# Layer 1 of an expert mixture: the picks in the last 32 key rows done as plain products over their 4096 experts instead of gathered

## The reference

```python
def peer_ffn(h, w_query, sub_keys, u_tab, v_tab):          # per 128 tokens
    q = (hc @ w_query).reshape(128, 8, 2, 64)               # 8 heads, 2 halves
    s = jnp.einsum('chpd,hpnd->chpn', q, sub_keys)          # 128 scores a half
    s_top, i_top = lax.top_k(s, 16)
    cand = s_top[:, :, 0, :, None] + s_top[:, :, 1, None, :]
    cand_id = i_top[:, :, 0, :, None] * 128 + i_top[:, :, 1, None, :]
    best, pos = lax.top_k(cand, 16)                         # 16 experts a head
    eid = take_along_axis(cand_id, pos)                     # 128 experts a token
    gate = softmax(best)
    act = gelu(einsum('chkd,cd->chk', u_tab[eid], hc)) * gate
    return einsum('chk,chkd->cd', act, v_tab[eid])
```

## Time and profile before

| What | us |
|---|---|
| Median of three runs | 3532.21 (3530.38 to 3534.53) |
| Span of the profiled execution | 3317.3 |
| Median less that span, outside the recorded work | 214.9 |
| PE busy | 2336.2 (70%) |
| DVE busy | 1679.4 (51%) |
| POOL busy | 1480.8 (45%) |
| ACT busy | 558.5 (17%) |

### The profile page before, as it was taken

The page is one execution under the profiler, slowest core; times in us unless marked ns, Lnnn a source line. Parts: engine busy times, 40 slices in busy tenths (PEclk is TensorE's granted clock), DMA queues, the critical chain, the costliest instruction groups (busy, mean ns, idle before and its releaser), DMA issues.

```text
span 3317.3 us, 36982 instructions
## 1 busy us (share of the span) xinstructions
PE 2336.2 (70%) x12540; PEld 1281.0 (39%) x12540; DVE 1679.4 (51%) x4368; ACT 558.5 (17%) x1179; POOL 1480.8 (45%) x1577
## 2 busy tenths in 40 slices
PE   7899867898999888995465444447898545444444
PEld 5477624365777545764121000004587400000000
DVE  2521576644233586436965444443712795444444
ACT  2320231401100235102240000002511210000000
POOL 1100044444444444430666777771000167777775
PEclk9999978799999898997575555557899755555555
DMA  8967679899999896991999999993233299999998
GB/s 307 352 209 267 238 269 350 304 354 378 362 365 366 323 347 235 363 334 64 375 349 388 409 409 409 409 409 111 70 114 134 84 379 409 409 409 406 409 409 341
DMA packets 325915, 1047.22 MB, mean 316 GB/s; under 512 B 27424, under 2 KB 38752, under 8 KB 325728
## 3 DMA queue, kind: packets, MB, share of 16 engines
q0 software_dynamic: 240192, 880.90, 69.2%
q1 hardware_dynamic: 85536, 163.95, 14.1%
HBM read 1043.70 MB, written 1.05 MB: 315 GB/s over the span
## 4 chain that ended last, share of the span: by engine, by line
PE 49%; DVE 18%; issue 13%; DMA 10%; ACT 3%; PEld 3%; POOL 2%; PEldq 0%; DVEq 0%; ACTq 0%; POOLq 0%
PE ps L404 24%; PE ps L440 12%; DVE UV L1044 8%; DMA UV<-in_v_tab,idxT 7%; PE ps L426 4%; PEld ps L404 3%; ACT arena L1679 2%; PE ps L396 2%; DMA W<-in_w_mod 2%; POOL UV L2157 1%; PE ps L529 1%; PE ps L571 1%; DVE arena L1415 1%; DVE arena L1424 1%; DVE arena L1418 1%
## 5 line engine op out<-in xcount | busy, mean ns | idle before, releaser
L1044 DVE SCALAR_TENSOR_TENSOR UV<-ps,UV 128x1024 f32<-128x1024 f32 x768 | 909.8, 1222 | 833.4 <-PE ps L426 816.3
L2157 POOL DMA_INDIRECT UV<-in_u_tab,idxT x768 | 723.5, 942 | 1182.4 <-DVEq L1510 498.1
L440 PE MATMUL ps<-UV,acts 128*32 128x512 f32 x3072 | 632.5, 908 | 560.3 <-DVE acts L1053 456.6
L2167 POOL DMA_INDIRECT UV<-in_v_tab,idxT x768 | 724.9, 944 | 281.6 <-issue 198.8
L404 PE MATMUL ps<-H,W 128*128 128x256 f32 (+2 forms) x3296 | 668.7, 363 | 36.4 <-ACT H L1679 26.5
L404 PEld LDWEIGHTS ps<-H,W 128*128 128x128 f32 (+1 forms) x3296 | 574.7, 194 | 147.3 <-issue 76.6
L404 PE MATMUL ps<-arena,W 128*128 128x256 f32 (+1 forms) x1632 | 371.6, 385 | 20.4 <-issue 8.6
L440 PEld LDWEIGHTS ps<-UV,acts 128*32 128x32 f32 x3072 | 78.3, 129 | 716.1 <-DVE acts L1053 572.7
L404 PEld LDWEIGHTS ps<-arena,W 128*128 128x128 f32 (+1 forms) x1632 | 304.4, 190 | 103.3 <-issue 53.2
L426 PE MATMUL ps<-hs,selb 32*128 32x512 bf16 x1536 | 208.5, 530 | 153.1 <-DVE UV L1044 153.0
L1679 ACT ACTIVATE gel<-dots 128x2 f32<-128x2 f32 x384 | 77.4, 202 | 1255.9 <-DVE UV L1044 1247.3
(11 more groups left out here) (198 smaller groups left out, 1698.9 us busy)
## 6 DMA issues: line engine op xcount, KB each, us to landing
W<-in_w_in SPq DMA_DIRECT2D x30, 2048.0 KB, 10.1
UV<-in_w_mod POOLq DMA_DIRECT2D x18, 2048.0 KB, 12.3
W<-in_w_ff SPq DMA_DIRECT2D x16, 2048.0 KB, 14.2
UV<-in_w_ada POOLq DMA_DIRECT2D x9, 2048.0 KB, 11.7
W<-in_w_out SPq DMA_DIRECT2D x8, 2048.0 KB, 11.4
W<-in_w_mod POOLq DMA_DIRECT2D x6, 2048.0 KB, 19.9
W<-in_w_query SPq DMA_DIRECT2D x6, 2048.0 KB, 9.2
UV<-in_u_tab,idxT POOLq DMA_INDIRECT x768, 8.8
```

Source lines behind the costliest of these rows:

```text
L440: last = mm(ps[q:q + GROUP, YB, :], acts[:, tok % SLOTS, GROUP - 1 - r:2 * GROUP - 1 - r], Vs[:, tok % SLOTS, hf * 512:(hf + 1) * 512], st ...
L1044: dve.scalar_tensor_tensor(out=Us[:, j, :], in0=ps[:, b:b + 2, :].rearrange("p a b -> p (a b)"), scalar=1.0, in1=Us[:, j, :], op0=MUL, op1 ...
L2157: pool.indirect_dma_start(Us[:, j, :], None, A["u_tab"], off).then_inc(sem(f"u_arrived{j}"), 16)
L2167: pool.indirect_dma_start(Vs[:, j, :], None, A["v_tab"], off).then_inc(sem(f"v_arrived{j}"), 16)
```

## The change

Key rows 96 to 127 of layer 1 (DROWS = 32, D0 = 96) are taken out of the gathers of tiles 4 and 5. For tokens from 512 on, both gathers get a bound: an index above it (experts 12288 and up of layer 1) is to be passed over without an error, and the slot keeps what it held. The gates used with the gathered rows are kept in two new tiles, gates_even and gates_odd, in which the gates of the passed-over picks are zero; gateT keeps the full gates. Since a slot may now hold old rows, `dot` no longer writes its product over them: its output goes to the PSUM banks that it read. This holds for all 768 tokens, the other layer too.

The passed-over picks are computed by a new function `dense`, placed after the routing of tile 5 and its rows, in front of `close_stream`. It has three parts.

1. Marks, 64 times for 4 tokens each. DVE builds a one-hot of each pick's second key (colhot, 128 by 4 by 128), a one-hot of its first key among the 32 rows (rowhot, 128 by 4 by 32), and multiplies the latter by the gates. PE multiplies the two (4 products), which gives for each token a 32 by 128 map of gates. After every 16 tokens ACT copies the maps, PE transposes them, and ACT writes them to G (128 experts of a row on partitions; 32 rows; 256 tokens).
2. Rows, 32 times. PE transposes the 128 experts of a key row of u_tab (8 transposes), ACT copies them, and PE multiplies them by H (8 products of 128 by 128 by 256). ACT takes the gelu of two rows at once and DVE multiplies by the map in G.
3. Outputs, in 4 quarters of 256 features. PE multiplies the rows of v_tab by G (32 products of 256 columns for each of two halves of a quarter, 256 in all), and DVE adds the sums to X.

The tables' last quarters come through the weight ring as 16 chunks of 2 MB: 8 of u_tab in rows of 4 KB, 8 of v_tab in pieces of 1 KB. Beats stand between all parts, with a pace of their own (DPACE = 3.2 us of estimated work a visit).

The core of the diff:

```diff
+DROWS = 32
+D0 = NKEY - DROWS
+DPACE = 3.2
@@ the chunks
+        def dense_chunks(tag):
+            at = LAYER[tag] * NEXP + D0 * NKEY
+            for c in range(DROWS // 4):
+                chunk(("du", tag, c), rows(A["u_tab"][at + 512 * c:at + 512 * c + 512, :]), 4, D)
+            for q in range(QUARTERS):
+                for c in range(DROWS // 16):
+                    chunk(("dv", tag, q, c), rows(A["v_tab"][at + 2048 * c:at + 2048 * c + 2048, :])[:, :, 256 * q:256 * q + 256], 16, 256)
@@ PE
+                for b in range(MARKS):
+                    pe.wait_ge(sem("picks_marked"), nxt("picks_marked"))
...
+                    for q in range(MARKED):
+                        last = mm(o[32 * q:32 * q + 32, b % 4 * P:(b % 4 + 1) * P], rowhot[:, b % 2, q, :], colhot[:, b % 2, q, :],
+                                  start=True, stop=True)
...
+                    dense_beat(0.9)
...
+                turn_rows_of(0)
+                for r in range(DROWS):
+                    if r + 1 < DROWS:
+                        turn_rows_of(r + 1)
+                    pe.wait_ge(sem("rows_turned"), nxt("rows_turned", 2))
...
+                    for k in range(DT):
+                        last = mm(o[:, r % 2 * SEQ:(r % 2 + 1) * SEQ], turned[r % 2][:, k, :], H[:, k, :], start=(k == 0), stop=(k == DT - 1))
...
+                    dense_beat(5.0)
...
+                        for e in range(2):
+                            for r in range(16):
+                                i = 16 * c + r
+                                last = mm(o[e][:, 0:SEQ], w[:, r, e * P:(e + 1) * P], G[:, i, :], start=(i == 0), stop=(i == DROWS - 1))
+                                if r == 7:
+                                    dense_beat(3.6)
...
+                            dense_beat(3.6)
+            dense("x1")
             close_stream(1)
@@ DVE
-                    dve.scalar_tensor_tensor(out=Us[:, j, :], in0=ps[:, b:b + 2, :].rearrange("p a b -> p (a b)"), scalar=1.0,
-                                             in1=Us[:, j, :], op0=MUL, op1=MUL, accum_out=dots[:, j:j + 1]).then_inc(sem("dots"), 1)
+                    both = ps[:, b:b + 2, :].rearrange("p a b -> p (a b)")
+                    dve.scalar_tensor_tensor(out=both, in0=both, scalar=1.0, in1=Us[:, j, :], op0=MUL, op1=MUL,
+                                             accum_out=dots[:, j:j + 1]).then_inc(sem("dots"), 1)
+                def mark(b):
...
+                    dve.tensor_tensor(out=colhot[:, b % 2, :, :], in0=iotak.unsqueeze(1).to_broadcast([P, MARKED, P]),
+                                      in1=colT[:, four].unsqueeze(2).to_broadcast([P, MARKED, P]), op=ALU.is_equal)
+                    link(dve.tensor_tensor(out=rowhot[:, b % 2, :, :], in0=iotak[:, D0:].unsqueeze(1).to_broadcast([P, MARKED, DROWS]),
+                                           in1=rowT[:, four].unsqueeze(2).to_broadcast([P, MARKED, DROWS]), op=ALU.is_equal))
+                    dve.tensor_tensor(out=rowhot[:, b % 2, :, :], in0=rowhot[:, b % 2, :, :],
+                                      in1=wide(gateT)[:, four].unsqueeze(2).to_broadcast([P, MARKED, DROWS]),
+                                      op=MUL).then_inc(sem("picks_marked"), 1)
@@ POOL
+            def bound(tok):
+
+                return {"bounds_check": NEXP + D0 * NKEY - 1, "oob_is_err": False} if tok >= 4 * P else {}
-                    pool.indirect_dma_start(Us[:, j, :], None, A["u_tab"], off).then_inc(sem(f"u_arrived{j}"), 16)
+                    pool.indirect_dma_start(Us[:, j, :], None, A["u_tab"], off, **bound(tok)).then_inc(sem(f"u_arrived{j}"), 16)
```

More of the change, by code:

```diff
@@ L234, in two_blocks_kernel @@
         hp2 = view(9232, D, dt=bf16)
+        G = view(0, DROWS, SEQ)
+        colhot = view(8192, 2, MARKED, P)
+        rowhot = view(9216, 2, MARKED, DROWS)
+        colT = view(9472, 2 * P)
+        rowT = view(9728, 2 * P)
+        iotak = view(9984, P)
+        turned = [view(8192 + 1024 * i, DT, P) for i in range(2)]
+        beside_g = [varb, rstd]
         NBANK, HB, YB = 8, 0, 4
@@ L468, in beat @@
                 owed[0] += us
-                while owed[0] >= PACE and seen[0] < min(segment[1], PAIRS * ready[0]):
-                    owed[0] -= PACE
+                while owed[0] >= pace[0] and seen[0] < min(segment[1], PAIRS * ready[0]):
+                    owed[0] -= pace[0]
                     visit(seen[0])
@@ L2041, in rows_after, with dense, dense_beat, copy_marks @@
                     beat("rows", n, s)
+            def dense(tag):
+                unit = counter()
+                def dense_beat():
+                    beat("dn", tag, unit("unit"))
+                def copy_marks(f):
+                    evac(("dm", tag, f), beside_g[f % 2][:, :])
+                    act.sem_inc(sem("marks_copied"), 1)
+                def set_marks(f):
+                    p = full_bank(act, ("dt", tag, f))
+                    link(A_(G[:, :, BLOCK * f:BLOCK * f + BLOCK], p.rearrange("p (t r) -> p r t", r=DROWS)))
+                    act.sem_inc(free(("dt", tag, f)), 1)
+                    act.sem_inc(sem("marks_set"), 1)
+                def copy_turned(r):
+                    if r > 1 and r % 2 == 0:
+                        act.wait_ge(sem("rows_scored"), nxt("rows_scored"))
+                    elif r > 1:
+                        full_bank(act, ("ds", tag, r // 2 - 1))
+                    for a in range(2):
+                        evac(("du", tag, r, a), wide(turned[r % 2][:, 4 * a:4 * a + 4, :]))
+                        act.sem_inc(sem("rows_turned"), 1)
+                def gelu_rows(i):
+                    if i > 1:
+                        act.wait_ge(sem("dense_acts"), nxt("dense_acts"))
+                    evac(("ds", tag, i), beside_g[i % 2][:, :], f=ACT.Gelu_apprx_tanh)
+                    act.sem_inc(sem("dense_gelus"), 1)
+                for b in range(MARKS):
+                    if b % 4 == 2 and b > 4:
+                        set_marks(b // 4 - 1)
+                    dense_beat()
+                    if b % 4 == 3:
+                        copy_marks(b // 4)
+                set_marks(MARKS // 4 - 1)
+                dense_beat()
+                copy_turned(0)
+                for r in range(DROWS):
+                    if r + 1 < DROWS:
+                        copy_turned(r + 1)
+                    if r and r % 2 == 0:
+                        gelu_rows(r // 2 - 1)
+                    dense_beat()
+                gelu_rows(DROWS // 2 - 1)
+                for _ in range(8 * QUARTERS * DROWS // 32):
+                    dense_beat()
             def first_norm():
```

126 lines of the change are left out of this document (121 added, 5 removed).

## The result

The changed kernel takes 3653.99 us (median of 4 runs, 3649.71 to 3661.51) against 3531.3 for the kernel before on the same chip: ratio 1.0365 [1.0343, 1.0387], 123 us slower. Forecast were +30, in a range that ended at 3635. The sign was right, the size was not.

What follows compares the result with a forecast made beforehand. Transfers were taken to bound the kernel before, with POOL 3% behind. Marks 121, rows 262, outputs 180 and tail 20 made 583 us against 553, +30: 3562 us, range 3526 to 3635 for 8 in 10.

Steps and rivals of the forecast that it cites:

- What bounds the kernel before: Closing 108 pairs: transfers fill the whole period, 5.12 us a pair; POOL's four gathers, 4.96 us, lie 3% below.
- the 214.9 us outside of it I leave as they are: Whole kernel: 214.9 us of the time lie outside the profiled span and stay, so span 3347 becomes 3562 us.
- Gathers: Layer 1, bounded gathers: transfers drop to 3.71 us a pair; POOL stays at 1.24 us a gather, floor 4.96 a pair.
- the upper bound of 1.34: POOL's time for a bounded gather: at most 0.10 us above 1.24, for a costlier test of each index.
- Rival A: Gathers in rows and outputs: POOL's work shrinks with the rows moved, 0.98 us a gather; 3535 us, chance 0.18.
- Rows: 32 dense rows with 51 visits: POOL 253 us, PE 245, DMA under 230, plus 9 for misfits: 262 us.
- Outputs: Dense outputs with 35 visits: POOL 174 us, PE 166, DMA 171 to 220; taken as 180 us.
- The price of 50 us for pieces of 1 KB: Outputs' table loads, 16.8 MB in 1 KB pieces: 41 us by bytes, 90 by packets, 50 taken.
- Marks: 64 marks at 1.16 us with 18 visits at 2.46 us, DVE working in order: 121 us.
- Dot product to PSUM: DVE's dot product written to PSUM: no difference taken, at most 0.1 us an instruction.
- rival C: Rows and outputs: PE's clock falls to 0.8 (sign: below 0.9 in the rows); 3622 us, chance 0.12.
- D: Gathers: POOL gets slower, 1.34 us a gather, 5.36 a pair; 3595 us, chance 0.10.

Runs made afterwards that it cites:

- e09_before_again: The kernel before, unchanged, profiled on a late chip (single gathers come late): 3556.94 us in its one run.
- e17_idle_bound: The kernel before with a bound on every gather that no index exceeds, so all rows move; late chip: ratio 1.0031 against the kernel before.
- e01_before: The kernel before, unchanged, profiled on a quick chip (409 GB/s): 3330.53 us, span 3328.8.
- e07_gelu_first: The changed kernel with ACT taking the GELU of two scored rows before copying the next turned row; late chip: ratio 1.0289 against the kernel before.
- e16_after_again: The changed kernel, unchanged, run on a quick chip: ratio 1.0299 against the kernel before.
- e15_gelu_first_again: The changed kernel with ACT's GELU ahead of the next turned row's copy, run on a quick chip: ratio 1.0248 against the kernel before.
- e02_bound_only: The changed kernel without its dense part, keeping bounded gathers, zeroed gates and dot product in PSUM; quick chip: ratio 1.0024 against the kernel before.

## Why the prediction was wrong, step by step

**What bounds the kernel before: right for its profile, wrong for the times.** The transfers fill the pair in the profiled execution. The 5.12 us were 553 us over 108 pairs, but 107 steps lie between the first dot products of pairs 276 and 383, 5.18 us each; no term of the forecast's sum rests on the difference. The times shown were of a late chip, where single gathers set the pair. The step "the 214.9 us outside of it I leave as they are" failed: 2 us lie outside, and the rest is inside, 70 us of it behind the first dot product of pair 276 (642.3 us to the end in e09_before_again and 642.4 in e17_idle_bound, 571.9 in e01_before). The gap of 6% between span and median was itself the hint that the profile was taken under other conditions than the times.

**Gathers: right in kind, the floor too low.** Passed-over rows cost the engines almost nothing, and POOL becomes the floor. But 1.24 us was taken as unchanged where it is 1.295; the upper bound of 1.34 held it. Over 86 pairs of rows and outputs that is 19 us. Rival A is out: with rows passed over a gather takes more than before, not less. The Trainium skill (DMA: Bandwidth & Descriptors, section SWDGE vs HWDGE vs iDMA) ties GpSimd's work to descriptors it computes; here the trace shows no such dependence: a gather costs 0.99 us whether it moves all its rows (e17_idle_bound) or 72% of them.

**Rows: this step failed, 262 against 310 and 356 us.** It compared totals, POOL 253, PE 245, DMA under 230, took the largest and added 9 us "for each load or wait of PE's that misfits". On the quick chip the parts are: POOL's floor 264 in place of 253 (the measured 262 without loads has no misfit in it at all); the loads 30; ACT's order 17. The DMA engines had time for the loads on average, as the sum said, but a load does not wait for the gaps: it delays the gathers beside it, and a POOL at its floor never gives that back. And the 2 us stop for the scored bank was in the diff (one bank, and a copy of the next row ahead of the GELU that frees it), not in the sum, which knew of no such dependence. On the late chip, as an estimate from runs on three chips: 51 x 5.84 = 298, and with the 30 of the loads it makes 328, what e07_gelu_first shows; ACT's order adds 28 to 37. How the loads cost there was not measured.

**Outputs: 180 against 191 and 235.** On the quick chip POOL's floor is 181, without loads the stage takes 186.5 (183 with half the products) and with them 192; the bound of 171 to 220 held. The price of 50 us for pieces of 1 KB was beside the point, since the loads cost the stage 5. On the late chip 35 x 5.84 = 204; less 5 for loads, some 25 us are left that no run took apart.

**Marks: 121 against 128 and 137.** The work was right to a few us; DVE's waits for spread between marks and visits were not in it.

**Dot product to PSUM: "no difference" cost 5 us.** The bound of 0.1 us an instruction covered it.

The balance for late chips: forecast +30; rows +94, outputs +55, marks +16, end -2; less the 70 us by which the kernel before is dearer there in the same stretch: +123. Measured +123. On the quick chip +30, +48, +11, +7 and -5 make +91; e16_after_again shows +100 by the medians and 92.5 between its span and that of e01_before.

Would a sound level have saved the range? That is within the noise: its upper end was 3635 / 3532 = 1.029, and the quick chip gave 1.0299 [1.0277, 1.0321]. The sign set for rival C did appear on late chips (a clock of 0.86 in the rows, below the 0.9 that was named; 0.93 on the quick chip), but its mechanism did not: with half the products the clock fell to 0.79 and the rows took 322 us against 328. D was right in kind and half right in size: POOL got slower by 0.055 us a gather, not 0.10, and that explains 19 us of the miss.

No version beat the kernel before. The nearest with the dense part whole, e15_gelu_first_again, is 2.5% slower. The reason is in e02_bound_only: the change frees 27% of a resource behind which, 3% away, stands another that it slows, and pays for it with new work that takes 380 us by itself (80.5 + 184.8 + 114.0, ACT's order included) and must be hidden beside 108 pairs.

## What to carry to other kernels

Before you free a full resource, take the next one's period from the timeline and price what the edit does to that one: here 3% was the whole prize, and the edit's own bound test ate it. When two streams share a resource, do not compare totals with a maximum; ask which of them is in order at its floor, because it adds every delay that the other causes. And when the span and the timed runs differ by more than a few us, take it that the profile and the times come from different conditions, and look for the stretch that shows which.

## What was not expected of the hardware

- A gather with a bound costs POOL 0.99 us instead of 0.94, at any number of passed-over rows; each of these is still a packet, under 512 B.
- The same program has 409 or about 355 GB/s in the same stretch, each chip keeping its level in all its runs, and differs by 6% in its time. On the late chips DVE waits up to 10.9 us for a gather's rows, and the pair stays at 5.84 us with 27% of the bytes gone. Why is open.
- A load of 2 MB beside gathers delays the v rows in flight by up to 4.8 us. The Trainium skill (DMA: Bandwidth & Descriptors, section Issuing engines are not separate DMA queues) says that transfers of SP and GpSimd run on the same 16 engines and interleave; the trace agrees: during one load SP's packets took 56% of the 16 engines and the gathers' 42%.
- A dot product of 1024 elements on DVE takes 27 ns more when it is written to PSUM (1249 against 1222), and the read of its sum 58 ns more (141 against 83).
- With half its dense products PE ran the rows at a clock of 0.79 instead of 0.89: work taken off PE came back as slower work.
